# Routed experts: token rows moved by DMA through DRAM instead of by matrix products with selection matrices

## The chip, the cores and the metric

The program runs on one NeuronCore of a Trainium2 chip. Its engines are TensorE (PE in the profile, its weight loads PEld), VectorE (DVE), ScalarE (ACT), GpSimd (POOL) and SyncE (SP); sixteen DMA engines move data between DRAM and the on-chip memory. The metric is device time in microseconds, the median of several executions. Before the change three executions took 2874.83, 2875.08 and 2881.21 us; the median is 2875.08 us.

## What is computed

The program is a stack of transformer blocks over 256 tokens of width 1024, all in float32. The part that the change touches is the last layer: a mixture of eight experts. A router picks two experts for every token and weighs them; each expert is a gated feed-forward layer with its own three weight matrices.

```python
def moe_swiglu(h, w_router, w_gate, w_up, w_down):
    logits = jnp.einsum('bsd,de->bse', h.astype(F32), w_router.astype(F32))
    top_val, top_idx = lax.top_k(logits, TOP_K_EXPERTS)          # 2 of 8
    top_w = jax.nn.softmax(top_val, axis=-1)
    combine = jnp.sum(jax.nn.one_hot(top_idx, N_EXPERTS, dtype=F32) * top_w[..., None], axis=-2)
    out = jnp.zeros_like(h)
    for e in range(N_EXPERTS):
        out = out + combine[..., e:e + 1].astype(h.dtype) * swiglu(h, w_gate[e], w_up[e], w_down[e])
    return out
...
        x = x + gt2 * f          # gt2: a gate row of 1024 numbers
    return rms_norm_2(x, g_final)
```

Here h is the normalized x, scaled and shifted per column; w_gate[e] and w_up[e] are 1024 x 2816, w_down[e] is 2816 x 1024, 34.6 MB an expert and 277 MB in all. Everything else (attention of several kinds, five dense feed-forward layers, cross attention to a memory) comes before this layer and keeps its code, apart from one stretch of DMA that the change lays beside the dense layer of the third block.

## The kernel before

Every engine has its own program, written out in order, and they meet at semaphores. Weights come through a ring of seven slots of 1 MB: SP issues the transfer of weight unit u as soon as unit u-7 has been used (`slot_free`), and PE waits until unit u has landed (`unit_in`). `expert_units` lists the units of the expert layer: per expert 24 units of gate and up columns (function `gate_up`, three chunks i = 0, 1, 2 of 8 units; the units of chunk 2 are 0.75 MB and the others 1 MB) and 11 units of the down matrix (function `down`). The chunks are interleaved so that a `down` fills the time in which DVE and ACT make the hidden values of the chunk before it.

An expert has room for 96 tokens (CAP); a second path, `late_experts`, handles more and isn't entered here. Around the weights, PE does this for expert e:

- `gather` (L1106): the columns of the tokens that go to expert e are picked out of x by 16 matrix products with a 0/1 selection matrix `selr` (it carries the norm's root too), in two halves of 8, after units 1 and 3 of chunk 2 of the expert before. ACT copies them to `xg`, with the norm's scale and shift.
- `turn` (L1113): the selection matrix `sel` is transposed, two products, after unit 5 of chunk 2.
- `turn_hidden` (L1153): the hidden values are transposed, six products for each chunk.
- `scatter` (L1123): the result of expert e-1 (`ye`, 96 x 1024) is spread back over the 256 tokens by four products with the turned selection matrix, one after each of units 2 to 5 of chunk 1. DVE weighs each of the four pieces by the router's weight and adds it to `y` (L2852).

Before `scatter` the result has to leave PSUM: DVE copies 512 columns (L2875), ACT 256 (L1995), and GpSimd issues three transfers of 32 KB that bring the last 256 columns to their partitions (L887). After the last expert come its scatter, the product of `y` with half the gate row and the sum with x (L2935, L2936), then the final norm: squares on ACT (L1867), a power on GpSimd (L866), the scaling on DVE (L2768) and two stores of the output (L746).

## Time and profile before

| | value |
|---|---|
| median of three runs | 2875.08 us |
| the profiled execution, own time | 2867.15 us |
| its span, first to last instruction | 2865.4 us |
| mean granted TensorE clock | 0.985 of full speed |
| PE busy | 2758.6 us, 96% |
| DVE, ACT, POOL busy | 1104.8, 429.6, 160.3 us |
| moved by DMA | 607.88 MB, mean 212 GB/s |

The page gives busy time by engine and then cuts the span into 40 slices of 71.6 us. In its DMA row, a digit is the share of time in tenths in which the sixteen DMA engines were busy; below it stands what they moved. The expert layer fills the last eleven slices, its weight products run from 2063 us to 2838 us. The windows view gives, for a stretch of time, the busy time of PE, PEld, DVE, ACT and POOL with the number of instructions, then the granted clock, the DMA share (which can come out a little over 1) and GB/s. The chain of waits names, piece by piece, the work that set the end. "Landing" is the time from the issue of a transfer to its last byte.

### The profile page before, as it was taken

How to read it: one execution, taken by the hardware profiler on the slowest of the kernel's cores; microseconds unless marked ns; L12 is line 12 of the kernel's file. 1: busy time of each engine (PE TensorE's matmuls, PEld its weight loads, DVE VectorE, ACT ScalarE, POOL GpSimd, SP SyncE). 2: the span in 40 equal slices, each digit the busy share in tenths (PEclk: the TensorE clock that was granted, in tenths of full speed). 3: DMA queues.
4: the chain of work that ended last, by engine and by line, in shares of the span. 5: the costliest groups of instructions: out<-in, count | busy, mean ns of one | idle time of the engine just before them, and what ended most of it. 6: DMA issues, size and time to landing. Idle time of an engine off the chain costs nothing.

```text
span 2865.4 us, 46175 instructions
## 1 busy us (share of the span) xinstructions
PE 2758.6 (96%) x19612; PEld 1728.8 (60%) x19612; DVE 1104.8 (39%) x2519; ACT 429.6 (15%) x1174; POOL 160.3 (6%) x269
## 2 busy tenths in 40 slices
PE   8999899999999999999999999999899999999997
PEld 7875557787778545668866577856443444344433
DVE  4772332476567315235764354444311101101111
ACT  1010342010101013211012310113110111011100
POOL 3100100000000011000001000011000000000000
PEclk9999999999999999999999999999899999999998
DMA  7964323476566442336753144443299999999995
GB/s 238 328 213 152 120 72 105 162 256 223 184 219 234 148 146 88 118 118 206 243 161 121 59 163 148 169 110 114 103 350 361 363 352 348 373 357 361 343 371 182
DMA packets 303166, 607.88 MB, mean 212 GB/s; under 512 B 15104, under 2 KB 171936, under 8 KB 302832
## 3 DMA queue, kind: packets, MB, share of 16 engines
q1 hardware_dynamic: 287216, 550.79, 55.3%
q0 software_dynamic: 15744, 54.11, 5.5%
q8 instruction: 158, 2.59, 0.4%
q14 instruction: 48, 0.39, 0.0%
HBM read 603.00 MB, written 1.05 MB: 211 GB/s over the span
## 4 chain that ended last, share of the span: by engine, by line
PE 86%; issue 8%; DVE 3%; ACT 1%; DMA 1%; POOL 1%; DVEq 0%; SPq 0%; POOLq 0%; ACTq 0%
PE psum L1052 21%; PE psum L1139 16%; PE psum L1011 12%; PE psum L1179 8%; PE psum L1536 5%; PE psum L973 5%; PE psum L1274 3%; PE psum L1447 2%; PE psum L1557 2%; PE psum L997 1%; PE psum L1000 1%; PE psum L1106 1%; PE psum L1123 1%; PE psum L1662 1%; PE psum L1614 1%
## 5 line engine op out<-in xcount | busy, mean ns | idle before, releaser
L1139 PE MATMUL psum<-ring,xT 128*32 128x512 f32 (+1 forms) x4608 | 470.5, 560 | 1.6 <-ACT xT L1961 1.6
L1011 PE MATMUL psum<-ring,hid 128*128 128x512 f32 x880 | 386.7, 592 | 0.0
L1139 PEld LDWEIGHTS psum<-ring,xT 128*32 128x32 f32 x4608 | 143.9, 110 | 295.3 <-issue 294.0
L1011 PEld LDWEIGHTS psum<-ring,hid 128*128 128x128 f32 x880 | 164.8, 190 | 195.6 <-issue 195.6
L1179 PE MATMUL psum<-ring,proj 128*32 128x256 f32 x4224 | 232.3, 379 | 0.8 <-ACT proj L1987 0.8
L2862 DVE SCALAR_TENSOR_TENSOR proj<-proj,psum 128x256 f32<-128x256 f32 (+1 forms) x72 | 28.4, 395 | 500.4 <-ACT proj L1975 500.4
L973 PE MATMUL psum<-ring,xT 128*128 128x512 f32 (+1 forms) x480 | 200.1, 579 | 2.9 <-DVE xT L2250 1.5
L1179 PEld LDWEIGHTS psum<-ring,proj 128*32 128x32 f32 x4224 | 137.2, 110 | 99.6 <-issue 12.1
L1052 PE MATMUL psum<-xT,ring 128*128 128x128 f32 x1600 | 195.0, 275 | 0.0
L1052 PEld LDWEIGHTS psum<-xT,ring 128*128 128x128 f32 x1600 | 187.1, 192 | 0.3
L1536 PE MATMUL psum<-ring,xT 128*128 128x384 f32 (+1 forms) x448 | 157.6, 502 | 2.9 <-DVE xT L2205 2.9
L973 PEld LDWEIGHTS psum<-ring,xT 128*128 128x128 f32 x480 | 90.9, 190 | 110.0 <-issue 107.8
L1906 ACT ACTIVATE silu<-pT 128x256 f32<-128x256 f32 x100 | 41.8, 418 | 631.0 <-DVE pT L2693 440.2
L1274 PE MATMUL psum<-ring,memT 128*128 128x512 f32 x256 | 121.0, 612 | 7.0 <-issue 7.0
L1536 PEld LDWEIGHTS psum<-ring,xT 128*128 128x128 f32 x448 | 82.2, 191 | 61.9 <-issue 13.5
L1052 PEld LDWEIGHTS psum<-qT,ring 128*128 128x128 f32 x800 | 97.2, 192 | 23.9 <-issue 23.4
L1052 PE MATMUL psum<-diff_o,ring 128*128 128x128 f32 x800 | 97.5, 275 | 0.0
L1052 PE MATMUL psum<-qT,ring 128*128 128x128 f32 x800 | 97.4, 275 | 0.0
L1052 PEld LDWEIGHTS psum<-diff_o,ring 128*128 128x128 f32 x800 | 93.3, 192 | 0.0
L2563 DVE SCALAR_TENSOR_TENSOR proj<-proj,cols 128x256 f32<-128x256 f32 x168 | 81.3, 484 | 5.1
L2563 DVE SCALAR_TENSOR_TENSOR proj<-xn,cols,proj 128x256 f32<-128x256 f32 x168 | 81.3, 484 | 5.1
L1975 ACT ACTIVATE proj<-psum 128x256 f32<-128x256 f32 (+1 forms) x72 | 26.4, 367 | 370.0 <-PE psum L1139 370.0
(407 smaller groups left out, 3256.0 us busy)
## 6 DMA issues: line engine op xcount, KB each, us to landing
ring<-in_ffn_w_gu SPq DMA_DIRECT2D x88, 1024.0 KB, 6.5
ring<-in_w_exp_down SPq DMA_DIRECT2D x80, 1024.0 KB, 8.1
ring<-in_w_exp_gate SPq DMA_DIRECT2D x128, 512.0 KB, 6.7
ring<-in_w_exp_up SPq DMA_DIRECT2D x128, 512.0 KB, 8.6
ring<-in_ffn_w_down SPq DMA_DIRECT2D x44, 1024.0 KB, 9.4
xn<-in_w_ada POOLq DMA_DIRECT2D x24, 1024.0 KB, 8.6
proj<-in_w_ada POOLq DMA_DIRECT2D x24, 1024.0 KB, 9.1
ring<-in_w_exp_gate SPq DMA_DIRECT2D x64, 384.0 KB, 3.7
```

The lines of the kernel that those rows point to most:

```text
L973: ins = mm(banks[4 + 2 * s + b][:, 0:w], lhsT(k, b), wt[:, k - i * ks, :], start=(k == 0), stop=(k == KT - 1))
L997: mm(banks[4 + f][:, 0:S], gate[:, k, f * P:(f + 1) * P], xT[:, k, :], start=(k == 0), stop=(k == KT - 1))
L1011: ins = mm(banks[2 * b + h][:, :], hid[f][:, b * P:(b + 1) * P], rows[:, f, h * 512:(h + 1) * 512], start=first, stop=last, skip_group_che ...
L1052: ins = mm(banks[bank][:, t * P:(t + 1) * P], weights(t)[:, k, :], tokens[:, k, :], start=(new and t == 0 and k == 0), stop=(k == 3), skip ...
L1139: ins = mm(banks[g][32 * c:32 * c + 32, 0:2 * w], xg[e % 2][:, k, 32 * g:32 * g + 32], cols_[:, :, c * w:(c + 1) * w], start=(k == 0), sto ...
L1179: ins = mm(bank[32 * g:32 * g + 32, at:at + 256], tokens[:, 32 * tg:32 * tg + 32], wt[:, f, d0:d0 + 256], start=first and at == 0, stop=la ...
L1274: ins = mm(banks[7][:, :], memT[:, k, b * P:(b + 1) * P], slot(u).rearrange("p (k n) -> p k n", k=4)[:, k % 4, :], start=(k == 0), stop=(k ...
L1447: ins = mm(banks[4 + h % 2][:, t * S:(t + 1) * S], wt[:, k, t * P:(t + 1) * P], xT[:, k, :], start=(k == 0), stop=(k == KT - 1))
L1536: ins = mm(banks[(5, 7)[b]][:, 0:w], xT[:, k, b * P:(b + 1) * P], slot(u)[:, 0:4 * w].rearrange("p (k n) -> p k n", k=4)[:, k % 4, :], sta ...
L1557: ins = mm(banks[(7, 5, 0, 4)[n]][:, :], yTh[:, k, b * P:(b + 1) * P], slot(u).rearrange("p (k n) -> p k n", k=4)[:, k % 4, :], start=(k = ...
L1906: A_(silu[f][:, :].rearrange("p (b s) -> p b s", b=NB), values[f][:, 0, :, :], ACT.Tanh, scale=0.5)\
L2563: ins = V.scalar_tensor_tensor(acc, w, cols[:, 16 + k:17 + k], acc, ALU.mult, ALU.add)
```

## The change

Tokens are carried to their experts and back as rows of 4 KB in DRAM.

- Before the experts: every token has a place, slot 96e + rank for each of its two experts. DVE works the places out as integers (`places`), ACT makes `y` = x times the norm's root (two instructions of 128 x 1024), and GpSimd issues four indirect writes of 128 rows each to `token_rows`. For expert 0 alone the selection by products stays.
- For each later expert GpSimd issues one plain load of its 96 rows (`xrow_e`), and PE turns them with eight transposes (L1170) in place of the 16 products.
- `turn`, `scatter`, the additions into `y`, and the three 32 KB moves are gone. DVE takes the result out of PSUM with two products with half the gate row (`gate_tile`), and GpSimd stores it by two transfers to `result_rows`.
- After the last expert GpSimd fetches for each token its two result rows with four indirect loads of 128 rows, and DVE adds them to x, weighed, with four instructions of 128 x 1024. The final norm then runs for each block of 128 tokens by itself.
- `clear_rows`: beside the dense layer of the third block GpSimd writes zeros over the 768 slot rows and one spare row (seven transfers), so that slots without a token hold zeros.

```diff
+SLOTS = NEXP * CAP
+TOKEN_ROWS = SLOTS + NEXP * (S - CAP)
...
+        xrow_e = [vx[:, i, :] for i in range(2)]
+        gate_tile = diff_o[:, :, :].rearrange("p a n -> p (a n)")[:, 0:768]
+        taken = [[t.rearrange("p k s -> p (k s)")[:, i * D:(i + 1) * D] for i in range(2)] for t in (memT, kTx)]
...
+        token_rows = nc.dram_tensor("token_rows", (TOKEN_ROWS, D), F32, kind="Internal").ap()
+        result_rows = nc.dram_tensor("result_rows", (SLOTS + 1, D), F32, kind="Internal").ap()
...
+            def clear_rows(st):
+
+                pool.wait_ge(sm["norm_ssq"], 4 * st["n0"]["norm"])
+                link(nc.gpsimd.memset(zeros, 0.0))
+                for e in range(SLOTS // P):
+                    nc.gpsimd.dma_start(token_rows[e * P:(e + 1) * P, :].rearrange("p (a n) -> p a n", a=4),
+                                        zeros.unsqueeze(1).to_broadcast([P, 4, 256])).then_inc(sm["rows_out"], 16)
+                nc.gpsimd.dma_start(result_rows[SLOTS:SLOTS + 1, :].rearrange("p (a n) -> p a n", a=4),
+                                    zeros[0:1, :].unsqueeze(1).to_broadcast([1, 4, 256])).then_inc(sm["rows_out"], 16)
...
+                if st["kind"] == "ffn" and st["out"] == "gated":
+                    clear_rows(st)
...
+                    pool.wait_ge(sm["rows_out"], 16 * N_ZEROS)
+                    pool.wait_ge(sm["rows_scaled"], NB)
+                    pool.wait_ge(sm["chosen_ready"], 3)
+                    for b in range(NB):
+                        for m in range(2):
+                            nc.gpsimd.indirect_dma_start(
+                                out=token_rows[:, :], out_offset=bass.IndirectOffsetOnAxis(ap=place_i[:, 0, 2 * m + b:2 * m + b + 1], axis=0),
+                                in_=y[:, b, :], in_offset=None).then_inc(sm["rows_out"], 16)
+                    pool.wait_ge(sm["rows_out"], 16 * (N_ZEROS + 4))
                     for e in range(NEXP):
-                        t = ye[e % 2]
+                        if e + 1 < NEXP:
+
+                            pool.wait_ge(sm["gath_psum"], 2 * e)
+                            nc.gpsimd.dma_start(xrow_e[(e + 1) % 2][0:CAP, :], token_rows[(e + 1) * CAP:(e + 2) * CAP, :])\
+                                .then_inc(sm["rows_in"], 16)
+
+                        t, to = ye[e % 2], result_rows[e * CAP:(e + 1) * CAP, :]
                         pool.wait_ge(sm["ye_dve"], e + 1)
-                        pool.wait_ge(sm["ye_act"], e + 1)
-                        for g in range(GROUPS):
-                            nc.gpsimd.dma_start(t[32 * g:32 * g + 32, 768:D], t[96:P, 256 * g:256 * g + 256])\
-                                .then_inc(sm["ye_moved"], 16)
+                        nc.gpsimd.dma_start(to[:, 0:768], t[0:CAP, 0:768]).then_inc(sm[f"results_out{e % 2}"], 16)
+                        nc.gpsimd.dma_start(to[:, 768:D].rearrange("(g t) d -> t g d", g=GROUPS),
+                                            t[CAP:P, 0:768].rearrange("t (g d) -> t g d", g=GROUPS)).then_inc(sm[f"results_out{e % 2}"], 16)
+                    for i in range(2):
+                        pool.wait_ge(sm[f"results_out{i}"], 16 * NEXP)
+                    for b in range(NB):
+                        for m in range(2):
+                            nc.gpsimd.indirect_dma_start(
+                                out=taken[b][m], out_offset=None, in_=result_rows[:, :],
+                                in_offset=bass.IndirectOffsetOnAxis(ap=place_i[:, 1, 2 * m + b:2 * m + b + 1], axis=0))\
+                                .then_inc(sm[("rows_in", "last_rows_in")[b]], 16)
...
-                        pe.wait_ge(sm["sel_ready"], e + 1)
-                    if e:
+
+                    if e == 0:
+                        if half == 0:
+                            pe.wait_ge(sm["rows_scaled"], NB)
+                            pe.wait_ge(sm["chosen_ready"], 2)
+                        for k in range(4):
+                            for b in range(NB):
+                                ins = mm(banks[bank][:, k * CAP:(k + 1) * CAP], rows[:, b, 4 * half + k, :], sel[:, b, 0:CAP],
+                                         start=(b == 0), stop=(b == NB - 1))
+                    else:
+                        if half == 0:
+                            pe.wait_ge(sm["rows_in"], 16 * e)
                         pe.wait_ge(sm["gath_evac"], 2 * e + half)
-                    if e > 1:
-                        pe.wait_ge(sm["scat_read"], 4 * (e - 1))
-                    for k in range(4):
-                        for b in range(NB):
-                            ins = mm(banks[bank][:, k * CAP:(k + 1) * CAP], rows[:, b, 4 * half + k, :], selr[e % 2][:, b, 0:CAP],
-                                     start=(b == 0), stop=(b == NB - 1))
+                        for k in range(4):
+                            ins = nc.tensor.transpose(banks[bank][:, k * CAP:(k + 1) * CAP],
+                                                      xrow_e[e % 2][0:CAP, (4 * half + k) * P:(4 * half + k + 1) * P], ident[0:CAP, 0:CAP])
                     ins.then_inc(sm["gath_psum"], 1)
-
-                def turn(e):
-                    pe.wait_ge(sm["gath_evac"], 2 * min(e + 2, NEXP))
-                    for b in range(NB):
-                        ins = nc.tensor.transpose(banks[7][0:CAP, b * P:(b + 1) * P], sel[e % 2][:, b, 0:CAP], ident)
-                    ins.then_inc(sm["selT_psum"], 1)
-
-                def scatter(e, i, bank):
-                    b, h = pieces("b")[i]
-                    if i == 0:
-                        pe.wait_ge(sm["ye_moved"], 48 * (e + 1))
-                        pe.wait_ge(sm["selT_evac"], e + 1)
-                    elif bank == 7:
-                        pe.wait_ge(sm["scat_read"], 4 * e + i)
-                    mm(banks[bank][:, :], selT[0:CAP, b * P:(b + 1) * P], ye[e % 2][0:CAP, h * 512:(h + 1) * 512],
-                       start=True, stop=True).then_inc(sm["scat_ready"], 1)
...
-                    gate_up(e, 1, lambda k: scatter(e - 1, (2, 3, 4, 5).index(k), 7) if e and 2 <= k <= 5 else None)
+                    gate_up(e, 1, lambda k: None)
...
-                        if k == 5:
-                            turn(e)
...
-                    scatter(NEXP - 1, i, (0, 1, 2, 7)[i])
...
+                    act.wait_ge(sm["rsqrt_done"], st["root_of"])
+                    for b in range(NB):
+                        A_(y[:, b, :], x[:, b, :], ACT.Copy, scale=rs_col[:, st["rs"], b:b + 1]).then_inc(sm["rows_scaled"], 1)
...
+                    def select():
                         for b in range(NB):
-                            V.tensor_scalar(sel[e % 2][:, b, 0:CAP], C("slots")[:, 0:CAP], rank[:, b, e:e + 1],
-                                            chosen[:, b, e:e + 1], ALU.is_equal, ALU.mult)
-                            ins = V.tensor_scalar(selr[e % 2][:, b, 0:CAP], C("slots")[:, 0:CAP], rank[:, b, e:e + 1],
-                                                  chosen_rs[:, b, e:e + 1], ALU.is_equal, ALU.mult)
-                        ins.then_inc(sm["sel_ready"], 1)
-
-                    def gather_out(e, i, bank):
-                        b, h = pieces("b")[i]
-                        dve.wait_ge(sm["scat_ready"], 4 * e + i + 1)
-                        t = y[:, b, h * 512:(h + 1) * 512]
-                        if e == 0:
-                            V.tensor_scalar(t, banks[bank][:, :], comb[:, b, e:e + 1], None, ALU.mult).then_inc(sm["scat_read"], 1)
-                        else:
-                            V.scalar_tensor_tensor(t, banks[bank][:, :], comb[:, b, e:e + 1], t, ALU.mult, ALU.add)\
-                                .then_inc(sm["scat_read"], 1)
+                            ins = V.tensor_scalar(sel[:, b, 0:CAP], C("slots")[:, 0:CAP], rank[:, b, 0:1],
+                                                  chosen[:, b, 0:1], ALU.is_equal, ALU.mult)
+                        ins.then_inc(sm["chosen_ready"], 1)
+
+                    def places():
+                        spare = place[:, :, 1, :]
+                        V.tensor_tensor(place[:, :, 0, :], rank[:, :, :], C("expert_row").rearrange("p (b e) -> p b e", b=NB), ALU.add)
+                        link(V.scalar_tensor_tensor(spare, rank[:, :, :], float(CAP), C("spare_row").rearrange("p (b e) -> p b e", b=NB),
+                                                    ALU.is_ge, ALU.mult))
+                        link(V.tensor_tensor(place[:, :, 0, :], place[:, :, 0, :], spare, ALU.add))
+                        for m, rows in enumerate((m1, m2)):
+                            for b in range(NB):
+                                ins = V.tensor_tensor(rows[b], rows[b], place[:, b, 0, :], ALU.mult)
+                        link(ins)
+                        for m, rows in enumerate((m1, m2)):
+                            for b in range(NB):
+                                ins = V.tensor_reduce(place_sum[:, 0, 2 * m + b:2 * m + b + 1], rows[b], AX_X, ALU.add)
+                        link(ins)
+                        link(V.tensor_scalar(place_sum[:, 1, :], place_sum[:, 0, :], float(SLOTS), None, ALU.min))
+                        V.tensor_copy(place_i[:, :, :], place_sum[:, :, :]).then_inc(sm["chosen_ready"], 1)
...
+                            dve.wait_ge(sm[f"results_out{e % 2}"], 2 * 16 * (e // 2))
+                        V.tensor_tensor(ye[e % 2][:, 0:512], banks[5][:, :], gate_tile[:, 0:512], ALU.mult)
+                        V.tensor_tensor(ye[e % 2][:, 512:768], banks[6][:, 0:256], gate_tile[:, 512:768], ALU.mult)\
+                            .then_inc(sm["ye_dve"], 1)
...
-                    for b, h in pieces("b"):
-                        cut = slice(h * 512, (h + 1) * 512)
-                        link(V.scalar_tensor_tensor(y[:, b, cut], y[:, b, cut], 0.5, gate_rows[:, st["gate"], cut], ALU.mult, ALU.mult))
-                        V.tensor_tensor(x[:, b, cut], x[:, b, cut], y[:, b, cut], ALU.add).then_inc(sm["x_part"], 1)
+                    for b in range(NB):
+                        dve.wait_ge(sm[("rows_in", "last_rows_in")[b]], (16 * (NEXP + 1), 32)[b])
+                        for m in range(2):
+                            ins = V.scalar_tensor_tensor(x[:, b, :], taken[b][m], stat[:, 28 + 2 * m + b:29 + 2 * m + b], x[:, b, :],
+                                                         ALU.mult, ALU.add)
+                            if m == 0:
+                                link(ins)
+                        ins.then_inc(sm["x_part"], 2)
```

PE in one expert of the middle, before the change (L1139 is `gate_up`, L1179 `down`): the last scatter of chunk 1, then `down`, `turn_hidden` and chunk 2 with the gather (p_sb is the selection matrix) and the turning of it.

```order
L1139 MATMUL psum<-ring,xT 32x512 x12
L1123 MATMUL psum<-proj,qT 128x512
L1139 MATMUL psum<-ring,xT 32x512 x24
L1179 MATMUL psum<-ring,proj 32x256 x96
L1153 MATMUL psum<-cst,proj 128x128 x6
L1139 MATMUL psum<-ring,xT 32x384 x24
L1106 MATMUL psum<-p_sb,x 128x96 x8
L1139 MATMUL psum<-ring,xT 32x384 x24
L1106 MATMUL psum<-p_sb,x 128x96 x8
L1139 MATMUL psum<-ring,xT 32x384 x24
L1113 MATMUL psum<-cst,p_sb 96x128 x2
L1139 MATMUL psum<-ring,xT 32x384 x24
```

The same place after the change (line numbers have moved: L1187 is `gate_up`, L1226 `down`, L1201 `turn_hidden`, L1170 the transposes of the loaded rows in vx).

```order
L1187 MATMUL psum<-ring,xT 32x512 x96
L1226 MATMUL psum<-ring,proj 32x256 x96
L1201 MATMUL psum<-cst,proj 128x128 x6
L1187 MATMUL psum<-ring,xT 32x384 x24
L1170 MATMUL psum<-cst,vx 128x96 x4
L1187 MATMUL psum<-ring,xT 32x384 x24
L1170 MATMUL psum<-cst,vx 128x96 x4
L1187 MATMUL psum<-ring,xT 32x384 x48
L1226 MATMUL psum<-ring,proj 32x256 x96
```

Chunk 1 is one unbroken run of 96 products, the two groups of eight are two groups of four, and the two turns before the last units are gone.

GpSimd, the end of the program before the change: the last two experts' 32 KB moves and the root of the final norm.

```order
L887 DMA proj<-proj 32x256 [waits ye_act,ye_dve]
L887 DMA proj<-proj 32x256 x2
L887 DMA proj<-proj 32x256 [waits ye_act,ye_dve]
L887 DMA proj<-proj 32x256 x2
L866 TENSOR_TENSOR rs_col<-mean,minus_half 128x2 [waits mean_sq]
```

GpSimd after the change, first where the experts begin: the four indirect writes, the first load of rows and the first result's stores.

```order
L923 DMA token_rows<-y,place_i 2048x1024 [waits chosen_ready,rows_scaled,rows_out]
L923 DMA token_rows<-y,place_i 2048x1024 x3
L931 DMA vx<-token_rows 96x1024 [waits gath_psum,rows_out]
L936 DMA result_rows<-proj 96x768 [waits ye_dve]
L937 DMA result_rows<-proj 32x3x256
```

And at the end: the last load of rows, the last two results' stores, the four indirect fetches and the two roots.

```order
L931 DMA vx<-token_rows 96x1024 [waits gath_psum]
L936 DMA result_rows<-proj 96x768 [waits ye_dve]
L937 DMA result_rows<-proj 32x3x256
L936 DMA result_rows<-proj 96x768 [waits ye_dve]
L937 DMA result_rows<-proj 32x3x256
L943 DMA memT<-result_rows,place_i 128x1024 [waits results_out1,results_out0]
L943 DMA memT<-result_rows,place_i 128x1024
L943 DMA kTx<-result_rows,place_i 128x1024 x2
L896 TENSOR_TENSOR rs_col<-mean,minus_half 128x1 [waits mean_sq] x2
```

GpSimd's queue now holds, for each expert, two stores that wait for DVE and behind them the next load of rows; at the end four fetches stand behind the stores and wait for them to land.

## Rows read from the trace of the kernel before

**Rows 1.** The page: span, busy time, and the slices of DMA and GB/s.
```profile
span 2865.4 us, 46175 instructions
PE 2758.6 (96%) x19612; PEld 1728.8 (60%) x19612; DVE 1104.8 (39%) x2519; ACT 429.6 (15%) x1174; POOL 160.3 (6%) x269
...
PEclk9999999999999999999999999999899999999998
DMA  7964323476566442336753144443299999999995
GB/s 238 328 213 152 120 72 105 162 256 223 184 219 234 148 146 88 118 118 206 243 161 121 59 163 148 169 110 114 103 350 361 363 352 348 373 357 361 343 371 182
```

**Rows 2.** One expert by windows: engine busy us, granted clock, DMA share, GB/s.
```profile
2269.60:2367.05 97.45, 97.45 (x1168) 41.85 (x1164) 11.73 (x29) 9.64 (x26) 1.48 (x3) 1.00 0.99 359
```

**Rows 3.** The chain of waits in that expert: start us, us, what.
```profile
2286.04 1.06 PE psum L1123 x2
...
2314.05 0.81 PE psum L1153 x6
...
2318.86 1.96 PE psum L1106 x16
...
2330.78 0.35 PE psum L1113 x2
...
2346.31 20.74 PE psum L1139 x192
```

**Rows 4.** Waits of SP's queue in 2060 to 2860: total us, times, longest.
```profile
SPq L689 <- PE psum L1139: 232.2, 104, 30.0
```

**Rows 5.** DMA in that expert, 2.44 us a slice; issues with us to landing.
```profile
GB/s 355 404 407 412 409 366 406 409 412 409 410 402 403 301 337 301 289 299 326 294 338 363 193 397 313 390 358 353 392 417 419 407 412 405 412 409 388 190 217 240
...
DMA packets 10065, 34.98 MB, mean 359 GB/s; under 512 B 1016, under 2 KB 1016, under 8 KB 10056
...
ring<-in_w_exp_gate SPq DMA_DIRECT2D x8, 384.0 KB, 3.6
```

**Rows 6.** DMA from 2240 to 2290, 1.25 us a slice.
```profile
GB/s 400 416 400 416 419 416 416 397 406 410 413 410 416 406 403 410 400 370 206 206 246 190 190 236 364 416 410 397 406 406 413 413 406 398 343 390 413 410 406 413
```

**Rows 7.** The up-weights' transfers (L690), whole program: least, median, most.
```profile
DMA to landing us min/median/max: 3.7/7.8/14.7
```

**Rows 8.** Windows at the first expert's start, as in rows 2.
```profile
2060.00:2065.00 5.00, 3.42 (x26) 2.24 (x29) 0.00 (x0) 2.32 (x7) 0.00 (x0) 0.84 0.00 0
2065.00:2070.00 5.00, 5.00 (x40) 1.64 (x36) 0.00 (x0) 0.00 (x0) 0.00 (x0) 0.80 0.21 44
```

**Rows 9.** Timeline before the first gather: start us, us, engine and operation.
```profile
2054.58 0.33 DVE L2839 TENSOR_SCALAR p_sb<-cst,rank,chosen 128x96 f32<-128x96 f32 x1
...
2055.75 5.77 PEld L1106 LDWEIGHTS psum<-p_sb,x 128*128 128x128 f32 x32 [1.83 <-issue]
```

**Rows 10.** Timeline of the end, from the last expert matmul on.
```profile
2838.21 0.69 DVE L2875 COPY proj<-psum 128x512 f32<-128x512 f32 x1 [18.42 <-PE psum L1179]
2839.19 1.48 POOL L887 DMA_DIRECT2D proj<-proj  x3 [72.06 <-DVE proj L2875]
...
2857.73 0.63 ACT L1867 ACTIVATE xn<-x 128x512 f32<-128x512 f32 x1 [0.60 <-DVE x L2936]
...
2858.93 0.72 POOL L866 TENSOR_TENSOR rs_col<-mean,minus_half 128x2 f32<-128x2 f32 x1 [18.27 <-DVE mean L2175]
2859.69 2.48 DVE L2768 SCALAR_TENSOR_TENSOR xn<-x,rs_col,grow 128x1024 f32<-128x1024 f32 x2 [0.84 <-POOL rs_col L866]
2861.00 1.55 SPq L746 DMA_DIRECT2D out<-xn  x2
```

**Rows 11.** GpSimd's DMA issues of 128 partitions (L813): ns least/median/most.
```profile
L813 POOL DMA_DIRECT2D xn<-in_w_ada x24: 884/884/955, 33.8 to 1431.2; - x24
```

**Rows 12.** Landing of the 32 KB moves (L887), us.
```profile
DMA to landing us min/median/max: 1.7/5.1/5.9
```

**Rows 13.** A window of the dense layer, columns as in rows 2.
```profile
1710.00:1740.00 30.00, 30.00 (x218) 25.46 (x217) 11.18 (x23) 3.54 (x9) 0.00 (x0) 1.00 0.59 195
```

130 lines of the change are left out of this document (63 added, 67 removed).

## The prediction

> **What bounds the kernel now.** I read the page first. PE is busy 96% of the span, and in the expert layer, the last eleven slices, the DMA engines too are marked at 9 tenths [rows 1]. So two engines may bound this layer, and the windows view of a single expert does not separate them: 97.45 us with PE busy for all of them, the clock at its full level (1.00, 2.4 GHz), and a DMA share of 0.99 [rows 2]. The waits do. SP's queue spends 232.2 us in that line alone waiting for PE to free a slot [rows 4], while PE's own waits in the loop hold no entry for a landing of weights. PE bounds the layer and DMA follows it. The chain of waits of one expert is PE and nothing else; [rows 3] shows one instance of each piece that isn't a weight product.
>
> How far behind PE the DMA engines are is the question of this case. While PE streams, a unit of 1 MB costs it 20.74 / 8 = 2.59 us [rows 3], which is 405 GB/s, and the slices of such stretches stand at 402 to 419, mean 409 [rows 5]. So the weights stream about as fast as PE can take them, and whatever PE does besides them is the time in which DMA catches up. In the middle of the expert it does: the slices fall to 289 to 363, and a transfer of chunk 2 lands after 3.6 us, which is an empty queue [rows 5]. At another place it loses: for some 7.5 us of each expert the rate is about half, 190 to 246 GB/s [rows 6], behind the two transfers of 64 partitions each that end a down matrix. There the longest landing is 14.7 us [rows 7]. A freed slot is asked for again after six more units, 6 x 2.59 = 15.5 us, so the margin is 0.8 us.
>
> **The start of the layer.** DVE makes two of the four selection tiles that come before the first gather; the four start 0.24 us apart (first at 2054.58, PE's first load at 2055.75 [rows 9]), so 0.5 us goes. ACT's two scalings (four of 512 columns cost 0.63 us each [rows 10], so about 2.5 us) run while DVE works on the router, about 8 us. The places, some 15 tiny instructions, and `gate_tile` are done on DVE while PE is in its first chunk. The four indirect writes carry 2 MB, 5.1 us at 409 GB/s. The DMA engines stand still just then, 0 GB/s from 2060 to 2065 and 44 to 2070, since all seven slots are full [rows 8]. I take them at nothing; were this cover gone, 5 us of queue would meet the first expert.
>
> **PE in the loop.** Per expert, from [rows 3]: four scatters at 1.06 = 4.2 us gone, in seven experts 29.6. Two half gathers at 1.96 = 3.9 become eight transposes; six of `turn_hidden` cost 0.81, so eight cost 1.1 (at most the products' own price, 8/16 of 3.9 = 2.0), saving 2.85, in seven experts 19.9. Two turns 0.35, eight times 2.8. Together 52.3 us, and an expert of the middle takes PE 97.45 - 7.4 = 90.0 us. DVE loses its additions and gains two products, ACT loses two copies; both are far from full [rows 2]. No new wait of PE is late: the row load of an expert is issued right after the store of the result before, some 30 us ahead of its transposes, and lands in well under that even from a loaded queue [rows 7].
>
> **DMA in the loop.** An expert moves 34.98 MB [rows 5]. The change takes 0.10 off (the three moves) and adds a load and a store of 96 rows of 4 KB, 0.79: 35.67 MB. At 409 GB/s that is 87.2 us. The half-rate stretch costs more on top: with one slice at either side, eight of 1.25 us hold 2008 where 3272 would stand, 3.9 us [rows 6]. Sum 91.1 us, that is 1.1 more than PE needs. So here the bound changes hands, by little. PE then waits at weights. The first time, the store and the load (1.9 us) come at the end of the half-rate stretch, beyond the margin of 0.8: 1.1 us. Then 1.1 for each of six more experts: 7.7 us in all. The bounds: nothing, if the rate when PE pushes is 415 instead of 409 (86.0 + 3.9 = 89.9); at 400 GB/s (89.2 + 3.9 = 93.1) 3.1 x 7 = 22 us.
>
> **The end.** Now it is 27.2 us from the last weight product at 2838.2 to the end of the span at 2865.4. After: two products out of PSUM, 0.69 as the copy [rows 10] and about 0.4, and the gap to GpSimd 0.3: 1.4. Two store issues at 0.5 (1.48 / 3 [rows 10]): 2.4. Landing 1.7, the least [rows 12], plus 0.39 MB at 409, 1.0: 5.1. Then four indirect fetches. No row shows one. Below, a plain small issue, 0.5 us; far above, each waiting out a landing of 5.9 [rows 12]. I take 0.9, GpSimd's issue of a 128-partition load [rows 11], the row nearest in kind: issued by 8.9 us, landed with 0.5 MB at 11.9. DVE adds two rows of 1024 per block at 1.28 (2.48 for two [rows 10]); the first block starts at about 10, the second ends at 15.1. Squares of 1024 columns 1.3, mean and power 1.1, scaling 1.3, and 3.2 from the end of the scaling to the end of the span [rows 10]: 22.0. That gains 5.2 us. With 0.5 an issue it gains 7; with 5.9 it loses 15.
>
> **The zeros.** 3 MB in pieces of 1 KB join the dense layer, where PE is full and the DMA share is 0.59 [rows 13]; at the slowest rate seen, 190 GB/s, they are 16 us of transfer, spread over slots that PE needs only every 6 us or so. Nothing, and at most a few us if they all queue ahead of one unit.
>
> **Sum.** -0.5 - 52.3 + 7.7 - 5.2 = -50.3 us. The profiled execution's own time is 2867.15 (span 2865.4), so it would be 2816.9. The median before is 2875.08, 7.9 above the profiled one; with the same difference the median comes to 2824.8, forecast 2825.
>
> **A rule against it.** The trace shows weights arriving at 402 to 419 GB/s over tens of microseconds [rows 5, 6], yet over a whole expert 359 [rows 2]. The Trainium skill, page "DMA: Bandwidth & Descriptors", section Bandwidth, holds that for transfers between HBM and SBUF the HBM side of about 358 GB/s a core is what binds; its page "HBM Reference", Specifications, adds that a core alone goes well above this, to about 425. By the first, an expert would take 35.67 / 0.358 = 99.6 us and the kernel would be slower. The slices agree with the second.
>
> **Rivals.**
> A, the forecast: chance 0.52, own range 2815 to 2836.
> B, DMA keeps up and PE gets all it saves: 2825 - 7.7 = 2817. For it, the empty queue in chunk 2; against it, the margin of 0.8 us. 0.15.
> C, the end is dear: indirect fetches cost 3 us of GpSimd each, so four add 8.4 and the end is no gain: 2833; at 5.9 each, 2845. Against it stands only that the plain issue is 0.9. 0.15.
> D, the weights can't be pressed closer: the mean of 359 over an expert is all that the memory gives, and the low slices of its middle are weakness, not rest. Then an expert takes 35.67 / 0.359 = 99.4 us, 1.9 more than now, seven times 13.5, with the start and end -5.7: about 2883, slower than before. It decides from a mean of 363 GB/s down (98.3 us an expert, where 0.8 x 7 eats the 5.7); the forecast needs 391. Against it, the landing of 3.6 us in that middle [rows 5]. 0.10.
> E, rows and weights disturb each other on the DMA engines, by 3 to 5 us an expert beyond their bytes (the half-rate stretch gets longer, since store and load fall into it): 2846 to 2860. 0.08.
>
> **How the numbers follow.** The range must hold 8 in 10: from 2812 (B with a rate of issue below mine) to 2850 (C whole, half of E). D stays outside. 0.3% of this kernel is 8.6 us, about what a measurement can tell from no change. Faster by more than that: A, B, C and E, 0.89. Within it: between E and D, 0.03. Slower: most of D, 0.08.
>
> **What would show it.** Chain and windows: period of an expert 91 us; 90.0 for B, 99 for D. PE's waits should name a landing in ring at `gate_up` just after the half-rate stretch, some 8 us in total; none would speak for B. The middle slices of an expert should rise from about 310 GB/s to near 400, and landings in chunk 2 from 3.6 us to above 6. L1170 at 0.54 us for four. At the end, 22 us from the last product to the end of the span, with GpSimd's fetch issues near 0.9 us. The forecast is wrong if the period stays at 97 or above, or if the end is longer than the 27 us of now.

## The result, and the profile after

The kernel takes 2854.11 us after the change (median of five executions, 2847.74 to 2857.74), against 2875.08 before: 21.0 us less, ratio 0.9923 with a 95% interval of 0.9908 to 0.9938. The interval lies below 1, so the kernel is faster, but by 0.8%, 21 us, where 50.3 us were forecast. The forecast was 2825, its range ended at 2850.

The page of the changed kernel, its lines as in [rows 1], and behind them the start of the chain that ended last:

```profile
span 2853.0 us, 45595 instructions
PE 2707.6 (95%) x19364; PEld 1706.8 (60%) x19364; DVE 1078.6 (38%) x2476; ACT 424.8 (15%) x1156; POOL 175.1 (6%) x285
...
PEclk9999999999999999999999999999899999999998
DMA  7964323476466542335754254443199999999996
GB/s 239 329 211 151 109 81 113 163 238 235 163 238 208 187 149 89 103 110 173 251 182 123 89 176 145 166 126 134 62 346 375 373 402 361 366 360 396 353 382 238
...
PE 79%; DMA 8%; issue 8%; DVE 4%; ACT 1%; POOL 1%; SPq 0%; POOLq 0%; DVEq 0%; ACTq 0%
```

PE lost 51 us of work (2758.6 to 2707.6), as it was meant to. The span lost 12.4. In the chain of the kernel before, PE had 86% and DMA 1%; now DMA has 8%. The work is gone and a wait stands in its place.

The profile of before that the prediction used had its experts earlier than any other profile of this case: the last norm ahead of them came at 2041.3 us, in the nine other profiles at 2048.3 to 2052.8, one of them that of the kernel before with a single transfer edited (experiment 7). The difference arises in code that the change doesn't touch, so the spans (-12.4) and the medians (-21.0) differ by it. The granted clock goes with it: ahead of that norm TensorE stood at 1.2 GHz instead of 2.4 for 44 us in the profile of before, for 65 us in that of the changed kernel and for 51 to 74 us in the other eight. By estimate, 21 us more at half the clock are worth about 10 us where TensorE sets the time. I therefore compare stretches within the experts. From the first to the last weight product of the layer it was 774.9 us (2063.3 to 2838.2) and is 754.0 (2072.5 to 2826.6): 20.9 less. That is nearly the whole result.

Three experts by windows, columns as in [rows 2], each from the start of the turning of one expert's last hidden values to the next one's:

```profile
2217.06:2312.22 95.16, 90.09 (x1132) 38.20 (x1132) 8.11 (x21) 8.87 (x24) 1.59 (x3) 1.00 1.03 379
2407.48:2504.65 97.17, 90.48 (x1131) 37.48 (x1132) 8.11 (x21) 8.87 (x24) 1.59 (x3) 1.00 1.02 372
2698.21:2789.23 91.02, 89.90 (x1132) 37.98 (x1132) 8.11 (x21) 8.88 (x24) 1.08 (x2) 1.00 1.02 380
```

Where [rows 2] had PE busy for all of 97.45 us, it now works 90 us of 95 to 97. The third window is the last expert, for which no further rows are loaded. Six periods, from one expert's row transposes to the next one's, take 90.36, 95.15, 95.26, 97.17, 95.67 and 97.90 us, mean 95.25: the gain is 2.2 us an expert, 13.2 in six, where the forecast had 6.4. The rest of the 20.9 lies outside these periods: 1.7 us ahead of the first transposes and 6.0 behind the last, where the experts end.

The waits of PE in the layer, 2050 to 2853, in us, times, longest:

```profile
PE psum L1226 <- DMA ring<-in_w_exp_down: 22.7, 15, 2.8
```

and before the gate and up products (page, part 5: busy us and mean ns, then idle us and what ended it):

```profile
L1187 PE MATMUL psum<-ring,xT 128*32 128x512 f32 (+1 forms) x4608 | 465.9, 559 | 10.8 <-DMA ring<-in_w_exp_up 9.2
```

That is 31.9 us of waiting for weights, where there was none. Counted from the row transposes at which a period begins, the waits stand at 45 to 88 us and none before that (one more comes at the very end of the layer). Of the 22.7 us ahead of down products 19.6 are in the three units that end a down matrix, which run during the half-rate stretch and just behind it, and 11.0 of these are ahead of the unit that comes in two halves. The largest, 2.8 us, is one of them, at 2276.1. The waits that the trace names are not all of the loss, since products that run short of weights are also recorded as longer: PE counts 90.1 to 90.5 us busy in the first two windows, where 89.2 are enough (experiment 1).

The DMA engines in the first of those windows, 2.38 us a slice, as in [rows 5]:

```profile
GB/s 389 399 397 395 404 411 412 403 406 412 405 405 413 413 394 412 410 408 412 300 203 193 212 207 356 410 405 408 417 307 387 403 408 412 410 412 405 392 405 401
...
ring<-in_w_exp_down SPq DMA_DIRECT2D x10, 1024.0 KB, 14.6
ring<-in_w_exp_gate SPq DMA_DIRECT2D x16, 512.0 KB, 11.5
ring<-in_w_exp_up SPq DMA_DIRECT2D x16, 512.0 KB, 15.1
ring<-in_w_exp_gate SPq DMA_DIRECT2D x8, 384.0 KB, 8.7
...
ring<-in_w_exp_down SPq DMA_DIRECT2D x2, 512.0 KB, 16.0
vx<-token_rows POOLq DMA_DIRECT2D x1, 384.0 KB, 8.0
```

The low slices of the middle, 289 to 363 in [rows 5], are filled, and the landing of 3.6 us there is 8.7: the queue no longer runs empty. The half-rate stretch (300 203 193 212 207 356) is still there, and it is longer: counted in slices of 1 us below 290 GB/s it was 7 to 10 us before (mean 8.7) and is 10 to 15 in the six experts (mean 12.8; 1 us or so depends on where the slices are laid). The mean rate in it is the same, 216 and 222 GB/s.

The end, with the columns of [rows 10]:

```profile
2826.59 0.69 DVE L2921 TENSOR_TENSOR proj<-psum,diff_o 128x512 f32<-128x512 f32 x1 [19.35 <-PE psum L1226]
...
2827.91 0.52 POOL L936 DMA_DIRECT2D result_rows<-proj  x1 [69.30 <-DVE proj L2922]
2828.41 0.55 POOL L937 DMA_DIRECT2D result_rows<-proj  x1
2833.57 1.03 POOL L943 DMA_INDIRECT memT<-result_rows,place_i  x1 [4.61 <-DMA result_rows<-proj]
2834.91 0.96 POOL L943 DMA_INDIRECT memT<-result_rows,place_i  x1 [0.30 <-issue]
...
2840.26 2.69 DVE L2980 SCALAR_TENSOR_TENSOR x<-memT,stat,x 128x1024 f32<-128x1024 f32 x2 [12.64 <-DMA memT<-result_rows,place_i]
2842.88 2.67 DVE L2980 SCALAR_TENSOR_TENSOR x<-kTx,stat,x 128x1024 f32<-128x1024 f32 x2
```

From 2826.6 to the end of the span at 2853.0 it takes 26.4 us, 0.8 less than before, where 5.2 less was forecast.

### The profile page after: what moved, and what is told of

It is laid out like the page before. It is cut to its first block, busy times and chain, and to the rows that moved or that the text cites. A ratio compares the mean times of both kernels' runs of the same rounds, so it can differ in the third digit from the quotient of the medians.

```text
span 2853.0 us, 45595 instructions
## 1 busy us (share of the span) xinstructions
PE 2707.6 (95%) x19364; PEld 1706.8 (60%) x19364; DVE 1078.6 (38%) x2476; ACT 424.8 (15%) x1156; POOL 175.1 (6%) x285
## 4 chain that ended last, share of the span: by engine, by line
PE 79%; DMA 8%; issue 8%; DVE 4%; ACT 1%; POOL 1%; SPq 0%; POOLq 0%; DVEq 0%; ACTq 0%
PE psum L1110 21%; PE psum L1187 12%; PE psum L1069 12%; PE psum L1226 6%; PE psum L1579 5%; PE psum L1031 5%; DMA ring<-in_w_exp_up 5%; PE psum L1317 3%; DMA ring<-in_w_exp_down 2%; PE psum L1490 2%; PE psum L1600 2%; PE psum L1055 1%; PE psum L1058 1%; PE psum L1705 1%; PE psum L1657 1%
## 5 line engine op out<-in xcount | busy, mean ns | idle before, releaser
L1187 PE MATMUL psum<-ring,xT 128*32 128x512 f32 (+1 forms) x4608 | 465.9, 559 | 10.8 <-DMA ring<-in_w_exp_up 9.2
L1187 PEld LDWEIGHTS psum<-ring,xT 128*32 128x32 f32 x4608 | 144.6, 110 | 308.0 <-issue 271.1
L1226 PE MATMUL psum<-ring,proj 128*32 128x256 f32 x4224 | 235.0, 379 | 22.7 <-DMA ring<-in_w_exp_down 22.7
L1226 PEld LDWEIGHTS psum<-ring,proj 128*32 128x32 f32 x4224 | 141.8, 110 | 119.9 <-DMA ring<-in_w_exp_down 25.8
L2023 ACT ACTIVATE proj<-psum 128x256 f32<-128x256 f32 (+1 forms) x72 | 26.4, 367 | 380.1 <-PE psum L1187 380.1
## 6 DMA issues: line engine op xcount, KB each, us to landing
ring<-in_w_exp_down SPq DMA_DIRECT2D x80, 1024.0 KB, 13.2
```

Source lines behind the costliest of these rows:

```text
L1187: ins = mm(banks[g][32 * c:32 * c + 32, 0:2 * w], xg[e % 2][:, k, 32 * g:32 * g + 32], cols_[:, :, c * w:(c + 1) * w], start=(k == 0), sto ...
L1226: ins = mm(bank[32 * g:32 * g + 32, at:at + 256], tokens[:, 32 * tg:32 * tg + 32], wt[:, f, d0:d0 + 256], start=first and at == 0, stop=la ...
```

## The experiments

The theory T: the two transfers of 64 partitions that end each down matrix run at half rate and hold back the whole queue. The kernel before hid that, since PE was slow enough for DMA to catch up. The rivals put the loss on the added rows, on where they fall, on the source rows of those two transfers, or on the rate of the weights as such. Ratios are to the kernel before, timed on the same chip (median 2873.76 us of 7 beside experiments 1 to 4, 2871.71 of 15 beside 5 to 8).

**1. One transfer of 128 partitions.** The unit reads 256 rows that lie together, instead of four blocks of 64 rows (two for each half), so the bytes and the units stay as they were, and the products get the wrong rows.

```diff
-                        rows = down[at:at + 4 * w, :].rearrange("(f h r) d -> h r f d", f=2, h=2)
-                        for h in range(2):
-                            sp.dma_start(slot(u)[64 * h:64 * h + 64, :].rearrange("p (f d) -> p f d", f=2), rows[h, P:w])\
-                                .then_inc(full, 16)
+                        sp.dma_start(slot(u).rearrange("p (f d) -> p f d", f=2),
+                                     down[at:at + 2 * P, :].rearrange("(f p) d -> p f d", p=P)).then_inc(full, 16)
```

> The changed kernel, but the last unit of each down matrix comes in one transfer over 128 partitions (256 rows in one run of the matrix, so other rows than the reference's) in place of two transfers of 64 partitions. PE's waits for weights are about 32 us in the loop of the changed kernel, and the period of an expert is 95.2 to 97.9 us. Theory T (the stretch at half rate behind the 64-partition transfers, lengthened by the row store and load that fall into it, is what keeps the weights back): the stretch is gone, the period falls to PE's own 90 us, the waits below 5 us, the median by 30 to 36 us to 2818 to 2824. Rival R1 (rows on GpSimd's queue disturb the weights wherever they lie): the stretch of 5 us goes, the rest stays, period about 93, median about 2838. Rival R2 (the stream is simply pressed to its limit, the stretch is only where it shows): period 94 or more, median 2845 or more.

Measured: 2815.96 us, ratio 0.9802 (0.9785 to 0.9818), 38 us below the changed kernel (35 by the ratios), and even below the 2818 to 2824 of T. From the first to the last weight product it takes 715.2 us, against 754.0. Windows of two experts, then the DMA slices of the first (2.23 us each):

```profile
2218.94:2308.17 89.23, 89.23 (x1134) 37.86 (x1131) 8.12 (x21) 8.90 (x24) 1.59 (x3) 1.00 1.02 399
2575.87:2665.11 89.24, 89.24 (x1135) 37.87 (x1131) 8.11 (x21) 8.90 (x24) 1.59 (x3) 1.00 1.02 399
```

```profile
GB/s 352 381 400 402 382 419 398 411 410 402 410 408 411 400 411 411 409 411 415 397 411 408 411 400 411 410 411 299 393 411 406 411 411 408 384 401 401 393 384 339
DMA packets 10145, 35.57 MB, mean 399 GB/s; under 512 B 992, under 2 KB 992, under 8 KB 10135
...
ring<-in_w_exp_gate SPq DMA_DIRECT2D x8, 384.0 KB, 6.1
...
vx<-token_rows POOLq DMA_DIRECT2D x1, 384.0 KB, 7.9
```

All six periods are 89.23 or 89.24 us with PE busy throughout, and PE waits for no weights. Rows are loaded and stored in each of them. So the loop's loss goes with the half-rate stretch, and 89.2 us is what PE needs for an expert. No slice is lastingly low.

**2. No rows in the loop.** The loop neither stores results nor loads rows; the transposes read rows that were loaded at its start, and the end fetches zeros.

```diff
-                        pool.wait_ge(sm["ye_dve"], e + 1)
-                        nc.gpsimd.dma_start(to[:, 0:768], t[0:CAP, 0:768]).then_inc(sm[f"results_out{e % 2}"], 16)
...
-                            pe.wait_ge(sm["rows_in"], 16 * e)
+                            pe.wait_ge(sm["rows_in"], 32)
```

> The changed kernel without row traffic inside the loop: two row loads before it (their rows serve all later experts), no stores of results (the result rows are zeros written beside the dense layer), so the output leaves out the experts' sum. PE, DVE and the weights as in the changed kernel. T: the stretch shrinks to what it was before the change (8 to 9 us of half rate), 88.8 us of DMA an expert, so PE bounds with 90 us: waits below 8 us, median 2820 to 2828. R1: the same, 2820 to 2828, since no rows are left to disturb. R2: period 93 to 95, median 2840 or more.

Measured: 2828.97 us, ratio 0.9844 (0.9828 to 0.9861), periods 89.24 to 94.79, mean 91.64. The DMA slices of the longest, 2309.4 to 2404.2 (2.37 us each):

```profile
GB/s 398 401 401 412 411 408 403 408 408 403 413 406 413 401 406 411 313 209 187 235 225 216 318 410 403 410 410 410 410 403 410 408 409 406 404 387 388 366 327 322
```

I had expected the stretch to shorten with the rows gone, to 8 or 9 us, and the median to be at most 2828. The stretch lasts 9 to 13 us (mean 11.7). So it gets longer without any rows, and the added rows can't be the main reason. That the fuller queue is, I infer: in the first of these periods, where PE still runs without a wait, the stretch is 9 us as before the change, and in the others, where PE waits, it is 11 to 13. Without the rows the two halves still cost 2.4 us an expert over the 89.23 of experiment 1; with the rows on top a period takes 3.6 us more, against 2.0 for their own 0.79 MB at 400 GB/s. From the first to the last weight product the difference is 19.2 us (754.0 against 734.8). The other 5 of the 25 us between the medians are at the end: with no stores to wait for it takes 21.4 us instead of 26.4.

**3. The rows at another place.** Store and load of an expert are issued after the transposes of the next, in chunk 2, away from the stretch.

```diff
+                        if e + 1 < NEXP:
+                            pool.wait_ge(sm["gath_psum"], 2 * (e + 2))
+                        if e:
+                            store(e - 1)
+                        if e + 2 < NEXP:
+                            load(e + 2)
```

> The changed kernel with store and load moved: both are issued after the transposes in chunk 2 of the next expert, some 40 us later than now, far from the stretch at half rate. Same bytes. T: the stretch is 8 to 9 us again, period about 92 to 93.5, median down by 15 to 25 us to 2829 to 2839. R1: the rows disturb as much there, period 95 to 96, median within 5 us of 2854. R2: also within 5 us of 2854.

Measured: 2850.39 us, ratio 0.9925 (0.9908 to 0.9943), mean period 94.27, the stretch 9 to 14 us (mean 11.2). A miss for what I expected: the stretch is now no longer than without rows, but by the ratio nothing is gained over the changed kernel (0.9923), and by the periods 1.0 us an expert. So the rows cost nearly the same wherever they stand. That the queue no longer has a place with spare time would explain it; no run shows it by itself.

**4. The halves in two queues.** GpSimd issues the second half of the pair, SP the first.

```diff
-                        for h in range(2):
-                            sp.dma_start(slot(u)[64 * h:64 * h + 64, :].rearrange("p (f d) -> p f d", f=2), rows[h, P:w])\
+                        sp.dma_start(slot(u)[0:64, :].rearrange("p (f d) -> p f d", f=2), rows[0, P:w]).then_inc(full, 16)
...
+                nc.gpsimd.dma_start(slot(u)[64:P, :].rearrange("p (f d) -> p f d", f=2), rows[1, P:w])\
```

> The changed kernel with the second of the two 64-partition transfers issued by GpSimd (its own queue), the first by SP as now, so that both halves can be under way at once. T, if two halves side by side run at the full rate: the stretch loses its half rate, period 90 to 91.5, median 2818 to 2828. T, if the two still go one after the other: no change, within 5 us of 2854. R1: 5 to 7 us better at most than the changed kernel times seven experts' stretch, about 2838, the rest stays. R2: 2845 or more.

Measured: 2845.16 us, ratio 0.9908 (0.9892 to 0.9925), mean period 93.14, the stretch 7 to 11 us (mean 9.7). The DMA slices of the period from 2312.6 to 2406.5 (2.35 us each):

```profile
GB/s 401 399 400 414 407 410 407 408 408 398 414 410 407 403 414 403 366 270 264 321 208 206 353 410 414 396 418 319 384 400 410 412 407 409 411 390 400 402 393 382
```

Neither of T's two cases is met, 2818 to 2828 or within 5 us of 2854. A part comes back, 2.1 us of 6.0 in the periods of its profile: a stretch at 264 to 321 GB/s and then one at half rate. How much is less sure than that: the profiled execution is the fastest of the four, and the ratio's interval overlaps that of the changed kernel. The layer takes 741.1 us in this profile, where it is 752.3 to 758.3 in the three kernels that issue the pair from one queue with the rows at their place (the changed kernel, experiments 6 and 8). Side by side the two halves overlap only partly.

**5. The same rows, fetched into 128 partitions.** This computes everything. GpSimd brings the unit by two indirect loads, each with a list of 128 row numbers: the two blocks of 64.

```diff
+    k = np.arange(2)[None, None, :] * 384 + (q // 64 * 192 + P + q % 64)[:, None, None] + CHUNKS[2][0]
+    put("tail_rows", k + np.arange(NEXP)[None, :, None] * FF)
...
+                for f in range(2):
+                    nc.gpsimd.indirect_dma_start(
+                        out=slot(u)[:, f * D:(f + 1) * D], out_offset=None, in_=A["w_exp_down_2"][0].rearrange("e r d -> (e r) d"),
+                        in_offset=bass.IndirectOffsetOnAxis(ap=tail_i[:, 2 * e + f:2 * e + f + 1], axis=0)).then_inc(sm["rows_out"], 16)
```

> The changed kernel with the last unit of each down matrix, the right rows this time, brought by two indirect fetches of 128 partitions and 0.5 MB each, issued by GpSimd, in place of SP's two transfers of 64 partitions. The whole computation is done. Theory T2 (transfers that reach only 64 partitions slow the whole queue; rows beside them are harmless): no stretch at half rate, period 89.2 us as with the single 128-partition transfer, no wait for weights, median 2814 to 2820. Rival R3 (it was the source: rows out of four places of the matrix, 0.75 MB apart, that memory gives slowly; the single transfer read 256 rows in one run): the stretch stays, period 93 to 96, median 2840 to 2855. Rival R4 (indirect fetches are slow beside a full weight queue): PE waits at this unit, some us an expert, median 2825 to 2850.

Measured: 2819.49 us (2812.68 to 2822.16), ratio 0.9814 (0.98 to 0.9829). Its interval lies wholly below that of the changed kernel (0.9908 to 0.9938), so it is faster than both kernels, with the whole computation done. An expert by windows:

```profile
2227.31:2316.55 89.24, 89.24 (x1135) 38.14 (x1131) 8.11 (x21) 8.85 (x24) 3.65 (x5) 1.00 1.02 399
```

The source rows are the scattered ones of the original, and the period is that of experiment 1; PE waits for no weights. So it was not the source (R3), and two transfers of 512 KB are harmless when each goes to 128 partitions. The reach of the transfer, 64 partitions or 128, is left as a cause.

**6. The other way round.** The rows of experiment 1, which lie together, in two transfers of 64 partitions.

```diff
-                        rows = down[at:at + 4 * w, :].rearrange("(f h r) d -> h r f d", f=2, h=2)
+                        rows = down[at:at + 2 * P, :].rearrange("(f h r) d -> h r f d", f=2, h=2)
```

> As the single-transfer experiment, the same 256 rows in one run of the matrix, but in two transfers of 64 partitions. T2: the stretch is back, 10 to 13 us an expert, period 93 to 97, time 2845 to 2857. R3: no stretch, period 89.2, time 2813 to 2820.

Measured: 2853.46 us, ratio 0.9937 (0.9919 to 0.9956), from two executions. One expert by windows, then its slices (2.45 us each):

```profile
2413.96:2511.77 97.81, 90.49 (x1134) 37.74 (x1130) 8.11 (x21) 8.87 (x24) 1.59 (x3) 1.00 1.02 367
```

```profile
GB/s 369 379 374 415 415 409 394 409 410 400 407 412 405 405 409 385 226 199 213 226 221 260 385 415 404 413 408 288 405 410 402 410 409 405 408 386 395 309 338 328
```

The stretch is back (226 199 213 226 221 260), 9 to 15 us an expert, and so is the mean period of 95.3. Experiments 1 and 6 differ only in one transfer to 128 partitions against two to 64 each: 37.5 us between their medians, 0.9802 against 0.9937 by the ratios.

**7. The kernel before with one transfer.** The edit of experiment 1 in the kernel before.

```diff
-                        for h in range(2):
-                            sp.dma_start(slot(u)[64 * h:64 * h + 64, :].rearrange("p (f d) -> p f d", f=2), rows[h, P:w])\
...
+                        sp.dma_start(slot(u).rearrange("p (f d) -> p f d", f=2),
+                                     down[at:at + 2 * P, :].rearrange("(f p) d -> p f d", p=P)).then_inc(full, 16)
```

> The kernel before, with the last down unit in one 128-partition transfer (other rows than the reference's). All theories: PE bounds there, the stretch costs nothing; period 97.45, median within 0.2% of the kernel before, 2868 to 2880. If it falls by 10 us or more, the unprofiled runs of the kernel before waited for weights though the profiled one did not. Also looked at: whether the part ahead of the experts, which took 2041 us in the profile of before and 2048 to 2051 in all others, is short here too.

Measured: 2874.92 us, ratio 1.0007 (0.9995 to 1.0019), all six periods 97.45. One expert by windows:

```profile
2328.32:2425.77 97.45, 97.45 (x1169) 41.85 (x1165) 11.73 (x28) 9.64 (x26) 1.47 (x3) 1.00 0.96 358
```

There the stretch cost nothing. So the same edit is worth 0 us in one kernel and 38 in the other: the change moved the bound onto it.

**8. Plain fetches at the end.** Each indirect fetch becomes a plain load of 128 rows, so the output sums the wrong rows. One execution, for its profile.

```diff
-                            nc.gpsimd.indirect_dma_start(
-                                out=taken[b][m], out_offset=None, in_=result_rows[:, :],
...
+                            nc.gpsimd.dma_start(taken[b][m], result_rows[(2 * m + b) * P:(2 * m + b + 1) * P, :])\
```

> The changed kernel with the four indirect fetches at the end replaced by four plain loads of 128 rows (the wrong rows). The end after the last weight product took 26.4 us in the changed kernel, where 22.0 was forecast; issue plus gap 1.26 us a fetch, landing 5.3 us. If being indirect is what costs, issue falls to 0.5 to 0.9 and landing to about 3, and the end to 22 to 24 us. If it is the 2 MB moved at that moment and the landing of the stores, it stays at 25.5 to 26.5.

Measured: 2859.75 us, from one execution, so its time is not compared. What follows the last product, as in the rows of the end above:

```profile
2832.36 0.69 DVE L2919 TENSOR_TENSOR proj<-psum,diff_o 128x512 f32<-128x512 f32 x1 [18.71 <-PE psum L1224]
...
2834.18 0.55 POOL L937 DMA_DIRECT2D result_rows<-proj  x1
2839.17 1.12 POOL L943 DMA_DIRECT2D memT<-result_rows  x2 [4.44 <-DMA result_rows<-proj]
2840.28 1.04 POOL L943 DMA_DIRECT2D kTx<-result_rows  x2
2844.71 2.69 DVE L2978 SCALAR_TENSOR_TENSOR x<-memT,stat,x 128x1024 f32<-128x1024 f32 x2 [11.33 <-DMA memT<-result_rows]
```

To the end of its span, 2857.4, this is 25.0 us against 26.4, so neither range of what I expected is met, 22 to 24 or 25.5 to 26.5; it is nearer to the second. A plain issue takes 0.53 to 0.59 us, an indirect one 0.93 to 1.03 and 0.30 of gap. That it is indirect costs the end about 1.3 us: with indirect fetches it takes 26.2 to 26.4 us in the four profiles with about such a wait for the stores (the changed kernel, experiments 1, 3 and 6). The larger part is the landing of the stores, 4.4 us of waiting here and 4.6 there, without which experiment 2 ends 5 us sooner. That wait is not the same everywhere: 4.3 to 4.6 us in the changed kernel and experiments 1, 3 and 6, but 2.8 and 2.9 in 5 and 4, whose ends take 25.5 us. After it come 5.5 us from the first plain fetch's issue to DVE's first addition.

## Why the prediction was wrong

**The step that failed** is "DMA in the loop", 91.1 us an expert. It measured 95.25. Split by the packets' times over six experts, slices of 1 us under 290 GB/s apart from the rest: 35.5 MB at 400 GB/s are 88.7 us, and the low slices lose 6.5, of which the half-rate stretch 5.7 and single slices elsewhere the rest. The forecast had 87.2 (35.67 MB at 409) and 3.9, all of it for the stretch. So 1.5 us is the rate, 400 where the good stretches of [rows 5] show 409 (with slightly fewer bytes), 1.8 is the stretch, and 0.8 are the single slices, which the forecast left out. The rate was inside my bounds (400 GB/s, 93.1). The stretch I took from [rows 6] as a constant and gave it no bound, although the change was to fill the very queue behind it. That, the single slices and a dearer end (below) are why 2854 lies outside a range that ended at 2850. Such a split adds up to the period whoever binds (experiment 1: 35.5 MB at 400 and 0.6 are 89.3), so it only shares out the time. That DMA binds is shown by PE's waits and by experiment 1. By the same count the stretch loses 3.9 us before the change, as forecast, 5.4 in experiment 2, 5.2 in 3 and 3.8 in 4.

In PE's account: from the first to the last weight product the forecast implies 774.9 - 52.3 + 7.7 = 730.3 us, and it took 754.0. The 23.7 between them and the 4.4 of the end are 28.1 of the 29.3 us that the forecast was off (50.3 - 21.0). Two errors stand in the 23.7. Late weights cost 754.0 - 715.2 = 38.8 us (experiment 1), not 7.7; and PE by itself needs 715.2, not 722.6, which gave 7.4 back.

**PE in the loop**: right in kind, and 0.8 us an expert too careful. An expert needs 89.23 us (experiments 1 and 5), forecast 90.0; L1170 takes 0.48 us for four, forecast 0.54. **The bound changes hands**: right, and the waits named a landing in the ring as said. Their place was only partly right: I had put them at `gate_up` just after the stretch, and 22.7 of the 31.9 us are ahead of `down`, most of them at the units of the stretch itself. The longest landing of the up-weights was 14.7 us [rows 7] and is 22.7, beyond the 15.5 after which a slot is wanted.

The transfers of the up-weights (L709), us:

```profile
DMA to landing us min/median/max: 4.5/12.8/22.7
```

**The reading of SP's waits** [rows 4] was weaker evidence than I took it for. SP still waits 212.0 us in the same line, though PE now waits for DMA:

```profile
SPq L708 <- PE psum L1187: 212.0, 104, 28.2
```

In experiment 1, where PE waits for nothing, it is 216.6. So this number hardly moves with the bound (232.2, 216.6, 212.0). What told the cases apart was PE's own waits.

**The start** and **the zeros**: right. The last norm ahead of the experts starts its power 9.5 us later than in the profile of before (2050.7 for 2041.3), PE's first load of the gather 9.1 later (2064.8 for 2055.75 [rows 9]): 0.4 us gained, forecast 0.5. The dense layer with the zeros takes 0.5 us more (1654.4 to 1879.0 before, 1663.5 to 1888.6 after), and experiment 2, which writes twice as many, reaches the experts earlier than any other of the nine (2048.3).

**The end**: 26.4 us, forecast 22.0. The first store issue came 1.3 us after the last product, as said. The first fetch could be issued at 7.0 us, forecast 5.1: I had given the stores a fixed part of 1.7, the least of [rows 12], where the median there is 5.1. The fetches take 1.26 us each with their gap, not 0.9, and DVE starts at 13.7, not 10: 4.4 us after the second fetch's issue, where I had counted about 3. What follows took 12.7 us, forecast 12.0.

**The rivals.** C, the dear end, was right in that the end gives nothing back, but at 1.26 us an issue and not 3. D is refuted: 399 GB/s over a whole expert in experiment 1, where 359 would have been the most. B's condition, no wait, is what experiments 1 and 5 restore: 2816 and 2819 for its 2817. That they meet it so closely is partly luck, since PE needed 7.4 us less than B had and the end 4.3 more. E gave the right size (2846 to 2860, a stretch that gets longer) and in the main the wrong reason: the stretch grows without any rows too (experiment 2). The rows do cost more than their bytes beside the halves, 3.6 us a period for 2.0. Without the halves no harm shows (experiment 1), but one of up to about 2 us an expert could hide there, since 35.6 MB at 409 GB/s take 87.0 of the 89.2 us.

**The clock.** The falls of the granted clock in the layer don't explain the loss. In the six periods of the changed kernel TensorE falls to 1.2 GHz once, for 3.4 us at 2673.8, just after a wait of 2.5 us; in experiment 2 twice, in its two longest periods (94.79 and 94.32), again just after a wait; in experiments 1 and 5 never. At the lower clock 48 products took 4.40 us instead of 2.80 (experiment 2, at 2363). Some 1.6 us in one period of six is far from the 6.0 that they lost on average.

**What the stretch is.** In it all sixteen DMA engines are busy (share 1.05 below). By the packet records of the changed kernel a packet of 4 KB takes about 300 to 370 ns (the middle half of them) from 2265 to 2272 us, where it took 162 (the median) from 2244 to 2261. So the engines are not idle, each is slower. The two stretches by windows:

```profile
2265.00:2272.00 7.00, 5.79 (x96) 2.79 (x92) 2.42 (x6) 1.13 (x3) 0.00 (x0) 1.00 1.05 202
2244.00:2261.00 17.00, 17.00 (x171) 5.73 (x166) 0.00 (x0) 1.03 (x3) 0.00 (x0) 1.00 1.02 408
```

The Trainium skill, page "SBUF — State Buffer", section "Door 1: The DMA port swizzle", says that partitions 0 to 63 are reached through only eight of sixteen ports, and 64 to 127 through the other eight. That would be half the rate of a full transfer, and the 193 to 212 GB/s beside 405 to 413 agree; which port a packet took, no trace shows. The Trainium skill's page "DMA: Bandwidth & Descriptors", section "Rules for kernel authors", says that two transfers to disjoint halves serialize and advises one of 128 partitions. Experiment 4, with the halves in two queues, agrees for the greater part: 3.9 of the 6.0 us stay. Here the two halves hold 1.05 MB, 5.2 us at 202 GB/s, but the low rate lasts 10 to 15 us, so other units must run slowly with them. How they get caught, and why a fuller queue catches more, no run settles.

## What to carry to other kernels

When work is taken off the engine that binds, ask which flaws of the next one were free until now. A low stretch in its trace need not be a constant of the transfer: here it grew from 8.7 to 12.8 us once the queue behind it was full, so bound that term upwards. A pair of 64-partition loads was worth 0 us before the change and 38 after it, more than the change itself gained. For a result that goes out to DRAM and is fetched again at once, count the landings and not the bytes: here 2.8 to 4.6 us of waiting on the way out, and 4.4 to 5.5 from a fetch's issue to its last byte on the way back.

## What the runs showed of the hardware that was not expected

- Two 64-partition transfers of 512 KB hold the DMA rate near 220 GB/s (mean of the slices under 290) for 7 to 10 us in the kernel before, whose queue has spare time, and for 10 to 15 us in the changed one, instead of the 5 us of their own bytes.
- An indirect fetch of 128 rows of 4 KB costs GpSimd 0.93 to 1.03 us and a gap of 0.30; in the middle of the stream, two of them bring a 1 MB unit with no loss against one plain transfer (period 89.23 or 89.24 in both).
- In experiment 1 the weights stream at 398 GB/s for six experts on end (535 us), with 0.79 MB of rows an expert among them, while PE is busy for all of the time.
